# A two-block transformer kernel: operands rounded in pairs of feature blocks, weights placed ahead of the modulation slabs in the ring, and the rotation on GpSimd

## The reference

```python
# first block, layer L = 0, 1
h = rms_norm(x, norm_w[L]);  proj = h @ w_in[L]        # 1024 -> 5376
q, k, v, z, q_h, f_h, i_h, g_h, gate_a, gate_h = split(proj)
q, k = partial_rope(q), partial_rope(k)                # the rotation: 16 of 64 features of 10 heads
a = sliding_window_attention(q, k, v, sinks) * silu(z)
logf, kin, qin = gates of f_h and q_h                  # decayed recurrence over chunks of 64
b = rms(hgrn2_recurrence(qin, kin, i_h, logf)) * silu(g_h)
x = x + (sigmoid(gate_a) * (a @ w_up_attn) + sigmoid(gate_h) * (b @ w_up_hgrn)) @ w_out
# then x = rms_norm(x, final_norm_w)

# second block, layer i = 0, 1
mod = silu(c) @ ada_w[i] + ada_b[i]                    # 1024 -> 6144: shifts, scales, gates
y = mixer(x * (1 + sc_t) + sh_t)                       # i = 0: top-k latent attention; i = 1: differential attention
x = layer_norm(ALPHA * x + (1 + g_t) * y)
y = square(relu(h @ w1)) @ w2                          # h = x * (1 + sc_c) + sh_c, 1024 -> 4096 -> 1024
x = layer_norm(ALPHA * x + (1 + g_c) * y)
```

## Time and profile before

| | us |
|---|---|
| median of three runs | 1302.39 |
| the profiled execution itself | 1302.41 |
| its span | 1300.7 |
| TensorE matmuls busy | 1109.9 (85%) |
| GpSimd busy | 746.5 (57%) |
| ScalarE busy | 547.9 (42%) |
| VectorE busy | 490.6 (38%) |

### The profile page before, as it was taken

The page is one execution under the profiler, slowest core; times in us unless marked ns, Lnnn a source line. Parts: engine busy times, 40 slices in busy tenths (PEclk is TensorE's granted clock), DMA queues, the critical chain, the costliest instruction groups (busy, mean ns, idle before and its releaser), DMA issues.

```text
span 1300.7 us, 15904 instructions
## 1 busy us (share of the span) xinstructions
PE 1109.9 (85%) x6584; PEld 939.7 (72%) x6584; DVE 490.6 (38%) x689; ACT 547.9 (42%) x748; POOL 746.5 (57%) x341
## 2 busy tenths in 40 slices
PE   4897988877978898699687999999789566999995
PEld 4786867666866676488565988886777455998994
DVE  4557352427572614144646201105300745201014
ACT  3555463335553643244442444443334433444441
POOL 4665554645654555365014788785558015788883
PEclk9898988988988988889798999999799567999997
DMA  5753533465535323863207567676596004565650
GB/s 203 247 182 139 194 114 114 172 217 198 191 128 177 115 97 130 289 214 99 97 13 246 187 235 256 229 244 212 207 337 230 33 0 130 174 198 179 195 163 32
DMA packets 101023, 221.58 MB, mean 170 GB/s; under 512 B 11361, under 2 KB 17879, under 8 KB 94807
## 3 DMA queue, kind: packets, MB, share of 16 engines
q1 hardware_dynamic: 95776, 210.29, 47.1%
q10 hardware_dynamic: 5174, 10.28, 2.2%
HBM read 219.48 MB, written 1.07 MB: 170 GB/s over the span
## 4 chain that ended last, share of the span: by engine, by line
PE 68%; DVE 12%; ACT 7%; DMA 6%; issue 4%; POOL 2%; SPq 0%; ACTq 0%; POOLq 0%; DVEq 0%
PE lin_ps L322 12%; PE lin_ps L323 12%; PE lin_ps L324 12%; PE tmp_ps L329 5%; PE tmp_ps L330 5%; PE tmp_ps L331 5%; PE tmp_ps L420 3%; PE lin_ps L329 2%; PE lin_ps L331 2%; PE lin_ps L330 2%; POOL wlo L810 2%; DMA ring<-in_w_in 2%; DMA ring<-in_b_w_in 2%; PE tmp_ps L517 2%; PE tmp_ps L377 2%
## 5 line engine op out<-in xcount | busy, mean ns | idle before, releaser
L810 POOL TENSOR_TENSOR wlo<-ring,whi 128x1024 fp32r<-128x1024 f32 (+2 forms) x304 | 727.4, 2404 | 439.6 <-ACT whi L887 437.3
L887 ACT CAST whi<-ring 128x1024 fp32r<-128x1024 f32 (+2 forms) x304 | 312.6, 1034 | 551.1 <-PE lin_ps L324 257.2
L322 PE MATMUL lin_ps<-whi,hThi 128*128 128x512 f32 (+2 forms) x528 | 215.0, 407 | 43.4 <-POOL wlo L810 11.5
L323 PE MATMUL lin_ps<-wlo,hThi 128*128 128x512 f32 (+2 forms) x528 | 209.6, 397 | 0.0
L324 PE MATMUL lin_ps<-whi,hTlo 128*128 128x512 f32 (+2 forms) x528 | 209.2, 396 | 0.0
L322 PEld LDWEIGHTS lin_ps<-whi,hThi 128*128 128x128 f32 x528 | 105.9, 201 | 76.3 <-issue 20.0
L329 PE MATMUL tmp_ps<-hThi,whi 128*128 128x256 f32 x520 | 149.9, 288 | 8.5 <-DVE hTlo L1534 8.5
L330 PE MATMUL tmp_ps<-hTlo,whi 128*128 128x256 f32 x520 | 149.1, 287 | 0.0
L331 PE MATMUL tmp_ps<-hThi,wlo 128*128 128x256 f32 x520 | 148.9, 286 | 0.0
L329 PE MATMUL lin_ps<-hThi,whi 128*128 128x256 f32 x352 | 104.2, 296 | 21.0 <-DVE hTlo L1176 9.0
L324 PEld LDWEIGHTS lin_ps<-whi,hTlo 128*128 128x128 f32 x528 | 105.5, 200 | 21.1
(11 more groups left out here) (245 smaller groups left out, 1475.8 us busy)
## 6 DMA issues: line engine op xcount, KB each, us to landing
ring<-in_mlp_w SPq DMA_DIRECT2D x64, 1024.0 KB, 5.3
ring<-in_ada_w SPq DMA_DIRECT2D x48, 1024.0 KB, 5.5
ring<-in_w_in SPq DMA_DIRECT2D x40, 1024.0 KB, 5.9
ring<-in_b_w_in SPq DMA_DIRECT2D x12, 1024.0 KB, 6.7
ring<-in_w_out SPq DMA_DIRECT2D x8, 1024.0 KB, 5.1
ring<-in_a_w_in SPq DMA_DIRECT2D x6, 1024.0 KB, 6.1
ring<-in_w_up_hgrn SPq DMA_DIRECT2D x4, 1024.0 KB, 5.9
ring<-in_w_up_attn SPq DMA_DIRECT2D x4, 1024.0 KB, 5.1
```

Of the source, the lines that this page charges most:

```text
L322: pe.matmul(ps, xh, hi, start=first, stop=False, skip_group_check=True)
L323: pe.matmul(ps, xh, lo, start=False, stop=False, skip_group_check=True)
L810: pool.tensor_tensor(wlo[:, n % PARTS, :, 0:width], ring[:, u % RING, 2 * h:2 * h + 2, 0:width], whi[:, n % PARTS, :, 0:width].bitcast(F32 ...
L887: act.copy(whi[:, n % PARTS, :, 0:width], ring[:, u % RING, 2 * h:2 * h + 2, 0:width]).then_inc(S("high_formed"), 1)
```

## The change

It has four parts.

- The operand in pairs. `high_of`, `low_of` and `mixed` work on two feature blocks at a time, each pair with its own semaphore, and TensorE waits for a pair in the half that first reads it.
- The order of the ring. At the four boundaries the first two units of the coming product are reserved ahead of the slabs, and the visit there has two slabs, without the closing of a group. The eight slabs that this takes from the boundaries go to four visits more: two in `s0` (behind misc and behind `q0`), and two in `s2` (behind v0 and behind v1; those behind q0, k0, q1 and k1 stay). Groups close behind these visits, or ahead of the last part of `out`.
- The rotation moves from VectorE to GpSimd, ahead of the low parts of the weights that stand behind level 3.
- TensorE waits for the operand behind, not ahead of, the wait for the weights.

```diff
+            def reserve(width, *parts):
+                reserved.append(len(halves))
+                unit(parts, width)
             def take_halves(width, *parts):
-                first = len(halves)
-                unit(parts, width)
+                if reserved:
+                    first = reserved.pop(0)
+                else:
+                    first = len(halves)
+                    unit(parts, width)
...
-            def operand_ready(first, second):
-                pe.wait_ge(*first)
-                rest.append(second)
-            def operand(k0):
-                if k0 and rest:
-                    pe.wait_ge(*rest.pop())
+            def operand_ready(*events):
+                rest.extend(events)
+            def operand(kk):
+                while rest and rest[0][0] <= kk:
+                    pe.wait_ge(*rest.pop(0)[1])
+            def turned(name, kk):
+                return (kk, (S("operand_mid"), bump("operand_mid"))), (kk + 2, read_of(name))
...
                 for k0 in (0, 4):
-                    operand(k0)
                     for r, hi, lo in take_halves(HALF, (slice(0, HALF), win(w, c0, HALF, k0))):
+                        operand(k0 + r)
...
+            def reserve_feat(w, c0):
+                for k0 in (0, 4):
+                    reserve(HALF, (slice(0, HALF), win(w, c0, HALF, k0)))
...
                 if L:
-                    ada(4)
+                    reserve_feat(w, F0)
+                    ada(2, close=False)
...
                     for c in range(2):
+                        if h and c:
+                            ada_close()
                         linear_part(f"f{L}out{c}", w_out, ...)
...
-            def mixed(name):
+            def mixed(name, first):
+                first()
                 if name in ADA_BOUNDARIES:
-                    ada(4)
+                    ada(2, close=False)
                 pe.wait_ge(S(f"{name}x"), 1)
                 feature_major(f"{name}hT", x)
-                operand_ready((S("mixed_low"), bump("mixed")), (S("mixed_low"), bump("mixed")))
+                operand_ready(*[(2 * j, (S("mixed_low"), bump("mixed"))) for j in range(4)])
...
                     half_used(mm, "s0misc", "s0ik")
+            ada(2)
             linear_feat("s0iq", w, 1280, hT)
-            ada_close()
...
                     linear_feat("s0q0", w, 0, hT)
+                    ada(2)
+                    ada_close()
...
-                    if n or part:
-                        ada(2)
                     linear_feat(f"s2{'qk'[part]}{n}", w, part * D + n * HALF, hT)
+                    ada(2)
             for n in range(2):
-                if n == 0:
-                    ada(2)
                 linear_tok(f"s2v{n}", w, 2 * D + n * HALF, HALF, hT)
+                ada(2)
...
+            def rotate(L):                 # GpSimd; gone from VectorE's lv == 5
+                lows(halves_at[f"f{L}lv3"][0] + 1, halves_at[f"f{L}lv3"][1])
+                pool.wait_ge(*read_of(f"f{L}kv"))
+                pool.wait_ge(*read_of(f"f{L}q"))
...
             pool.wait_ge(S("f_scaled"), 1)
+            rotate(0)
             rstd("f0h", st[:, 1], st[:, 2], "f0ho")
...
             def high_of(name, k0, cols=None):          # low_of on VectorE likewise, with operand_mid behind j == 0
                 ps = flat(full_tmp(name))
-                    ins = act.copy(flat(hThi[:, k0:k0 + 4, :]), ps)
+                for j in (0, 2):
+                        dst, src = flat(hThi[:, k0 + j:k0 + j + 2, :]), ps[:, j * T:(j + 2) * T]
+                        ins = act.copy(dst, src) ...
+                    ins.then_inc(S("operand_high"), 1)
...
             def mixed(name):                           # VectorE
-                for h in range(2):
-                    dve.wait_ge(*read_of(f"{name}hT{h}"))
-                    whole = flat(hs)[:, 4 * h * T:4 * (h + 1) * T]
-                    step(dve.tensor_copy(flat(hThi[:, 4 * h:4 * h + 4, :]), whole))
+                for k in range(0, KT, 2):
+                    if k % 4:
+                        dve.wait_ge(*read_of(f"{name}hT{k // 4}"))
+                    else:
+                        dve.wait_ge(S("mixed_mid"), bump("mixed_half"))
+                    whole = flat(hs)[:, k * T:(k + 2) * T]
+                    step(dve.tensor_copy(flat(hThi[:, k:k + 2, :]), whole))
```

More of the change, by code:

```diff
@@ L258, in used @@
                 return S("w_used"), value
+            reserved = []
+            def reserve(width, *parts):
+                reserved.append(len(halves))
+                unit(parts, width)
             def take_halves(width, *parts):
-                first = len(halves)
-                unit(parts, width)
+                if reserved:
[3 more added lines that the diff above has]
+                    unit(parts, width)
                 for h in range(2):
@@ L620, in _, with latent @@
             w = I["a_w_in_2"][0]
-            mixed("s0")
+            def latent(k0):
+                return 392, (slice(0, T), win(w, 1024, T, k0)), (slice(T, T + 8), win(w, 1856, 8, k0)), \
+                    (slice(264, 328), win(w, 1792, HD, k0)), (slice(328, 392), win(w, 1792, HD, k0))
+            mixed("s0", lambda: [reserve(*latent(k0)) for k0 in (0, 4)])
             ps = open_lin("s0misc")
@@ L624, in _ @@
             for k0 in (0, 4):
-                operand(k0)
-                for r, hi, lo in take_halves(392, (slice(0, T), win(w, 1024, T, k0)),
-                                             (slice(T, T + 8), win(w, 1856, 8, k0)),
-                                             (slice(264, 328), win(w, 1792, HD, k0)),
-                                             (slice(328, 392), win(w, 1792, HD, k0))):
+                for r, hi, lo in take_halves(*latent(k0)):
+                    operand(k0 + r)
                     for k in range(2):
@@ L821, in rstd @@
                 pool.tensor_tensor(y, v, power, ALU.pow).then_inc(S(f"{name}rstd"), 1)
+            def rotate(L):
+                lows(halves_at[f"f{L}lv3"][0] + 1, halves_at[f"f{L}lv3"][1])
+                pool.wait_ge(*read_of(f"f{L}kv"))
+                pool.wait_ge(*read_of(f"f{L}q"))
+                pool.wait_ge(S("trig"), 1)
+                for i in range(NT):
+                    heads = qkv[:, i, 0:640].rearrange("p (h d) -> p h d", h=10)
+                    x1, x2 = heads[:, :, 0:ROPE_HALF], heads[:, :, ROPE_HALF:2 * ROPE_HALF]
+                    sin, cos = (trig[:, i, c, :].unsqueeze(1).broadcast_to([P, 10, ROPE_HALF]) for c in range(2))
+                    pool.tensor_tensor(ropet[:, 0], x1, cos, ALU.mult)
+                    pool.tensor_tensor(ropet[:, 1], x2, sin, ALU.mult)
+                    pool.tensor_tensor(ropet[:, 2], x2, cos, ALU.mult)
+                    step(pool.tensor_tensor(ropet[:, 3], x1, sin, ALU.mult))
+                    pool.tensor_tensor(x1, ropet[:, 0], ropet[:, 1], ALU.subtract)
+                    step(pool.tensor_tensor(x2, ropet[:, 2], ropet[:, 3], ALU.add))
+                for i in range(NT):
+                    for a in range(2):
+                        ins = pool.tensor_copy(kdup[:, i, :, a, :], qkv[:, i, K0:V0].rearrange("p (g d) -> p g d", g=2))
+                ins.then_inc(S("f_rope"), 1)
             row, one = st[:, 1, :, 0], st[:, 2, :, 0]
@@ L1217, in ada_close, with ada @@
                          f"adaG{n}")
-            def ada():
-                ada_close()
+            def ada(close=True):
+                if close:
+                    ada_close()
                 name, slab = visits[visited[0]]
@@ L1637, in _ @@
                     dve.wait_ge(S("s0idx_used"), n + 1)
+                    if n == 1:
+                        ada()
+                        ada_close()
             ps = flat(full_tmp_of(dve, "s0ckvT"))
@@ L1690, in _ @@
             affine(1, "s2")
-            for _ in range(4):
+            for _ in range(6):
                 ada()
```

94 lines of the change are left out of this document (39 added, 55 removed).

## The result

The changed kernel takes 1289.79 us (median of 17 runs, 1284.59 to 1299.13) against 1302.77 for the kernel before on the same chip (17 runs, 1296.15 to 1309.96). The ratio is 0.9898, 95% interval 0.9879 to 0.9917: 13 us faster, where 26.9 were forecast.

A forecast was written before the change was run, and what follows sets the result against it. TensorE's own work was taken as the floor, its idle time as movable. Rotation -22.4, boundaries and operand waits, less +14.0 in s0 and +7.3 in s2, summed to -26.9 from 1302.4: 1276 predicted, range 1269 to 1283, wide 1264 to 1290.

The forecast's parts named there:

- Hidden: Levels: the rotation's sixteen GpSimd operations, 5.5 us, cost TensorE nothing, ahead of the low parts behind level 3.
- what this level waits for is VectorE alone: Level 6, layer 0: TensorE's 6.83 us wait is for VectorE's factors, not ScalarE's exponential; removing it gives -8.5.
- held up only by GpSimd's subtractions: Level 6, layer 0: without the rotation begun at 113.24, VectorE's factors can be ready by about 119.
- The prediction's signs of being wrong: Level 6 waiting for ScalarE, slabs late at a boundary, or idle time ahead of weights behind levels 3 and 4.
- the 0.3 given back: Levels, each layer: 0.3 us taken off the gain because the next level's buffer is read late.
- the smaller waits: Operand waits at f0f, both ua0, two bT operands and two projections: -5.4 us in all.
- The boundaries: Where x becomes an operand, first matmul earlier: s3 -1.75, s1 and s2 -2.9 each, layer 1 -3.7, s0 -9.1.
- s0 and s2: Four added visits and stalls lengthen s0 by 14.0 us (4.6 idle before iq), s2 by 7.3 (4.4 before k0).
- The levels have another bound: Rival: the level behind waits for ScalarE's exponential at 125.30, each layer gives back 5 us: 1286, chance 0.07.
- The rotation blocks GpSimd: Rival: at 2.43 us an operation, weights come late, TensorE waits 29 us per layer: 1334, chance 0.04.
- The ring gives back more: Rival: s0's boundary slabs land after x, or s2's six visits wait 2 us each, +12: 1288, chance 0.19.
- the rivals that it was widened for: Ring transfers later than forecast, 1288, chance 0.19; or two stalls of 4.5 us not arising, 1264, chance 0.16.

The follow-up runs named there:

- the one with three portions: Changed kernel, but GpSimd does the rotation in three portions, behind the low parts of levels 3, 4 and 5: 1285.3 us, ratio 0.9847.
- the one with both repairs: Changed kernel with rotation on VectorE behind the last level, s0's visit behind iq not misc, s2's behind q0 moved to s1: 1266.21 us, ratio 0.9717.

## Why the prediction was wrong

The direction and most terms held; one term failed, and at 14.8 us it is larger than all of the missing gain (13.9 between the forecast 26.9 and the 13 of the medians).

**The step that failed** is "Hidden", said of the rotation on GpSimd, and with it "what this level waits for is VectorE alone". Levels 3 to the last were to take 8.2 and 16.3 us less; they took 0.8 and 9.0 less. Of the 14.8 missing, 9.3 is what the rotation on GpSimd costs, the wait at level 4 with its half clock less the smaller wait that stands without it: the levels took 65.4 and 65.3 us with the rotation and 61.5 and 59.9 without. Its price on GpSimd was near enough (7.0 us for 5.5 forecast). What was wrong is whom it would make wait. I asked whether TensorE would wait for a low part, and it never did; VectorE waited, since the low parts that had been put off ran in one row beside the operations of level 4. The other 5.5 is the next bound: the wait of 2.0 ahead of level 6 in each layer, and 1.5 of half clock in layer 0. The prediction took the idle time of 6.83 as all to be had, with VectorE's factors ready by about 119, "held up only by GpSimd's subtractions". That leaves room for one low part. The four operations take 2.2 us without any (from 124.25 on in the kernel before); without the rotation they took 7.3 (114.99 to 122.26), the first 1.09 and two others 2.89 and 2.85.

Both could be read before. The trace of the kernel before shows VectorE's operations at two lengths, 0.68 and over 2 us. It also shows the rotation's own: 1.99, and its next one

```profile
115.15 2.43 DVE L1418 TENSOR_TENSOR ropet<-arena,trig 128x80 f32<-128x80 f32 x1
117.51 0.23 DVE L1419 TENSOR_TENSOR ropet<-arena,trig 128x80 f32<-128x80 f32 x1
```

where 80 elements take 2.43 us beside a low part and 0.23 without. I used this at s1 and s2, where it came out. The rule of the Trainium skill (SBUF — State Buffer, Who interferes with whom), that VectorE with two SBUF inputs and GpSimd take turns on the port by whole instructions, was cited there and not carried to the levels. These rows agree with it at both places. The Trainium skill (GPSIMD Engine Reference, Engine selection) has GpSimd about twice as slow for an elementwise product; alone an operation took 0.36 here against 0.23 on VectorE, 1.6 times.

The prediction's signs of being wrong (level 6 waiting for ScalarE, late slabs, idle time ahead of weights) did not show in the levels: the wait at level 4 was not among them. Its sum has two slips that change nothing: the 0.3 given back is taken once and not per layer (-22.1 in place of -22.4), and the smaller waits add up to 5.55 and not 5.4.

**The boundaries** held. s3: 11.94 us from VectorE's update of x to the first matmul, 11.8 forecast. s1 11.95 and s2 11.76, 11.8 forecast. Layer 1's boundary -4.2, -3.7 forecast. s0's -8.9, -9.1 forecast, with the slabs in time.

**The smaller operand waits** gave about 3 us where they were traced, of the 5.4: from the transposes to the first matmul f0f took 0.44 less (0.95 forecast), the two ua0 0.86 each (1.1) and s2's projection 0.87 (0.9), but s0's projection nothing (3.50 us in both), since its transposes ran at half clock.

**s0 and s2** held as sizes: s0 after its boundary +14.1 (+14.0), with 5.24 ahead of iq (4.6); s2 +9.0 (+7.3), with 5.22 ahead of k0 (4.4). The mechanism is shown by the two visits moved, which take both stalls away.

**The rivals.** "The levels have another bound", 1286, is the one that came nearest in place and price, with a chance of 0.07; its mechanism was the exponential and is not what happened. "The rotation blocks GpSimd" named the right engine, priced it at 29 us a layer and let it stall TensorE through the weights. "The ring gives back more" did not occur. The forecast's own range, 1269 to 1283, did not hold the time; the wide one, 1264 to 1290, held it at its very end, and that is luck, since the rivals that it was widened for are not what happened.

**Left open.** Whether the clock in s0's attention is lower because of what stands ahead of it, or by chance: the changed kernel had 0.50 for 40 us in one profile and 0.50 and 0.67 in another, and kernels with the same ring lay between 46.5 and 54.3 us for this stretch. And what the pairs are worth beside reserved units, 16 or 10.4: in the traces the four boundaries (1.71 each), layer 1 (2.4), the waits of the two ua0 (0.96 each), the two projections (0.97) and f0f (0.5) make 13.6.

## What to carry to other kernels

Work moved to an engine that seems idle must be asked two things: who waits for that engine's results, and who shares a resource with the instructions that it puts off. A gap in an engine is not free if what follows it then runs in one unbroken row beside another engine's chain; cut the moved work into pieces that fit the gaps one by one, or put it behind the critical loop on the engine where it was, which here was worth 10 to 14 us. The move to GpSimd in one piece gave 1.3 alone and 4 to 6 beside pairs and ring, and beside the ring without pairs it cost 1 (1.0009 to 1.0018), within the intervals. And when a wait is to be removed, look for operations just ahead of it that run at two lengths: the longer one is the next wait.

## What the runs showed of the hardware

- VectorE's operations on 512 elements with two SBUF inputs took 0.68 us alone, 0.84 when GpSimd ran operations on 80 elements in turn with them, and 2.8 beside a low part. In level 4 of the changed kernel each of four in a row waited for a low part of its own; none got ahead of the row.
- GpSimd's operation on 80 elements took 0.36 alone and 0.80 in turn with VectorE; four copies of 128 elements took 1.00 us in the changed kernel, 2.39 in the one with three portions and 2.84 in the one without the rotation.
- The price of one order of transfers: two slabs issued ahead of the second product's weights behind a boundary made 5.2 us of idle TensorE; issued one product later, none.
- The granted clock of TensorE in s0's attention, in two stretches of 20 us, was 0.50 and 0.50 in one profile of the changed kernel and 0.50 and 0.67 in the other; it was 0.70 and 0.79 in the kernel before, and 0.59 and 0.90 in the one with both repairs.
